# Six groups of value rows summed by TensorE, paired forgetting scores and a fifth late head in a hybrid attention and PEER block

## The reference

```python
h   = x + [ FoX(8 heads of 64) || DiffAttn(4 heads, two maps of 64) ](W_in RMSNorm(x)) @ W_out
h   = h + PEER(RMSNorm(h))
out = RMSNorm_final(h)

# PEER, for each token and each of its 8 heads:
q = (xb @ w_q).reshape(128, 8, 2, 128)            # a block of 128 tokens
sc = einsum('thpd,hpkd->thpk', q, sub_keys)       # two lists of 128 key scores
s1, i1 = top_k(sc[:, :, 0], 16); s2, i2 = top_k(sc[:, :, 1], 16)
top_s, pos = top_k(all 256 sums of s1 and s2, 16) # 16 of 16384 experts
g = softmax(top_s)
hid = gelu(einsum('thkd,td->thk', u_tab[eidx], xb)) * g
out = einsum('thk,thkd->td', hid, v_tab[eidx])
```

## Time and profile before

| | |
|---|---|
| median of 3 runs | 1542.28 us (1540.99 to 1546.88) |
| the profiled execution | 1541.62 us |
| its span, first to last instruction | 1539.8 us |
| TensorE busy | 1269.3 us, 82% |
| VectorE busy | 1077.6 us, 70% |
| ScalarE busy | 459.8 us, 30% |
| GpSimd busy | 751.5 us, 49% |
| DMA | 596.50 MB, mean 387 GB/s |
| granted TensorE clock, mean | 0.939 |

### The profile page before, as it was taken

The page is one execution under the profiler, slowest core; times in us unless marked ns, Lnnn a source line. Parts: engine busy times, 40 slices in busy tenths (PEclk is TensorE's granted clock), DMA queues, the critical chain, the costliest instruction groups (busy, mean ns, idle before and its releaser), DMA issues.

```text
span 1539.8 us, 13062 instructions
## 1 busy us (share of the span) xinstructions
PE 1269.3 (82%) x3727; PEld 658.2 (43%) x3727; DVE 1077.6 (70%) x2520; ACT 459.8 (30%) x1200; POOL 751.5 (49%) x637
## 2 busy tenths in 40 slices
PE   9999999988888488999787777677886787777778
PEld 7766655665545234444333333233332233332333
DVE  3247699999988867566666676666666766666654
ACT  3432355466343022222222222221222222222212
POOL 0016477675667443454544554445444554444440
PEclk9999999999989699999899999989999999999998
DMA  9669799997999999999999999999999999999995
GB/s 382 250 250 413 275 330 351 370 376 268 340 371 392 391 421 416 421 421 421 421 422 422 421 422 421 421 422 421 422 421 421 422 422 421 422 420 422 421 421 208
DMA packets 99741, 596.50 MB, mean 387 GB/s; under 512 B 11480, under 2 KB 11480, under 8 KB 42328
## 3 DMA queue, kind: packets, MB, share of 16 engines
q0 software_dynamic: 89856, 536.91, 86.0%
q1 hardware_dynamic: 9816, 58.77, 9.6%
HBM read 593.54 MB, written 2.10 MB: 387 GB/s over the span
## 4 chain that ended last, share of the span: by engine, by line
DMA 42%; PE 15%; DVE 6%; POOL 3%; issue 2%; ACT 2%; DVEq 0%; POOLq 0%
PE acc L994 13%; DMA map_mem<-in_peer_uv_dram,eidx 10%; DMA w_ring<-in_peer_uv_dram,eidx 9%; DMA v_all<-in_peer_uv_dram,eidx 7%; DMA act_mem<-in_peer_uv_dram,eidx 6%; DMA v_ring<-in_peer_uv_dram,eidx 3%; DMA mix_mem<-in_peer_uv_dram,eidx 3%; DMA u_ring<-in_peer_uv_dram,eidx 3%; DMA v_ring<-in_peer_v_dram,eidx 2%; PE mm L786 1%; ACT diag L1228 1%; DVE map_mem L1549 1%; DVE w_ring L1549 1%; PE sc L786 1%; POOL v_ring L692 1%
## 5 line engine op out<-in xcount | busy, mean ns | idle before, releaser
L1220 ACT ACTIVATE gel<-hid 128x4 f32<-128x4 f32 x126 | 25.8, 205 | 722.2 <-DVE hid L1549 712.5
L685 POOL DMA_INDIRECT u_ring<-in_peer_u_dram,eidx x112 | 136.8, 1221 | 172.9 <-DVE eidx L1529 99.5
L994 PE MATMUL acc<-v_all,diag 128*128 128x512 f32 x256 | 129.2, 651 | 61.1 <-ACT diag L1228 60.6
L692 POOL DMA_INDIRECT v_ring<-in_peer_v_dram,eidx x112 | 133.4, 1192 | 66.4 <-DVE h L1577 38.0
L1577 DVE SCALAR_TENSOR_TENSOR h<-v_ring,coef,h 128x1024 f32<-128x1024 f32 x112 | 143.9, 1284 | 14.3 <-DMA v_ring<-in_peer_v_dram,eidx 11.3
L994 PE MATMUL acc<-map_mem,diag 128*128 128x512 f32 x248 | 123.3, 644 | 32.0 <-ACT diag L1228 32.0
L994 PE MATMUL acc<-v_ring,diag 128*128 128x512 f32 x248 | 120.1, 629 | 32.3 <-ACT diag L1228 28.7
L1541 DVE CUSTOM_DVE_ANT_0 u_ring<-u_ring,hn 128x1024 f32<-128x1024 f32 x112 | 136.6, 1220 | 14.2 <-DMA u_ring<-in_peer_u_dram,eidx 14.0
L994 PE MATMUL acc<-u_ring,diag 128*128 128x512 f32 x248 | 119.1, 626 | 27.4 <-ACT diag L1228 25.8
L1228 ACT ACTIVATE diag<-ident,coef 128x128 f32<-128x128 f32 x392 | 126.3, 390 | 39.1 <-DVE coef L1567 30.8
L711 POOL DMA_INDIRECT v_all<-in_peer_uv_dram,eidx x64 | 76.1, 1189 | 92.3 <-PE acc L994 81.7
(11 more groups left out here) (281 smaller groups left out, 2331.9 us busy)
## 6 DMA issues: line engine op xcount, KB each, us to landing
w_ring<-in_slabs_dram SPq DMA_DIRECT2D x29, 1024.0 KB, 8.4
v_ring<-in_slabs_dram SPq DMA_DIRECT2D x6, 1024.0 KB, 11.2
u_ring<-in_slabs_dram SPq DMA_DIRECT2D x6, 1024.0 KB, 10.9
map_mem<-in_slabs_dram SPq DMA_DIRECT2D x6, 1024.0 KB, 7.9
h<-in_x_dram SPq DMA_DIRECT2D x4, 512.0 KB, 12.5
u_ring<-in_peer_u_dram,eidx POOLq DMA_INDIRECT x112, 6.9
v_ring<-in_peer_v_dram,eidx POOLq DMA_INDIRECT x112, 7.1
v_all<-in_x_cols_dram SPq DMA_DIRECT2D x3, 512.0 KB, 7.4
```

The costliest lines, as they stand in the source:

```text
L685: nc.gpsimd.indirect_dma_start(out=u_ring[:, c % U_RING, :], out_offset=None, in_=peer_u[0], in_offset=bass.IndirectOffsetOnAxis(ap=eidx[n ...
L692: nc.gpsimd.indirect_dma_start(out=v_ring[:, c % V_RING, :], out_offset=None, in_=peer_v[0], in_offset=bass.IndirectOffsetOnAxis(ap=eidx[n ...
L994: last = nc.tensor.matmul(acc[half][:, :], diag[:, c % COLS, :], v_row(n, c)[:, half * BANK:(half + 1) * BANK], start=first, stop=(n % PH ...
L1220: nc.scalar.activation(gel[:, par, g0:g0 + COLS], hid[:, par, g0:g0 + COLS], ACT.Gelu).then_inc(gelu_done, 1)
```

## The change

Three edits.

1. Six of the 28 groups (`SUMMED`, groups 4, 7, 10, 13, 16, 19) are no longer added row by row by VectorE. ScalarE makes four diagonal matrices of the group's coefficients (`sum_diag`), TensorE multiplies the four v rows with them into two of the three rotating banks, and VectorE adds the two banks to `h` (`add_sum`). The piece `sum` stands at gap 0 of slot k + 2; the bank adds stand at gap 1 of the next slot, or before the next output projection's add. The planner gives a sum a share of 10. `row_taken` says which semaphore tells that a v row has been used.
2. The forgetting scores of two neighbouring heads are issued together, at even steps: two products from partitions 0 and 64, then the two gate products.
3. `LATE_HEADS` is 5.

```diff
-LATE_HEADS = 4
+LATE_HEADS = 5
+SUMMED = (4, 7, 10, 13, 16, 19)
+SHARE_SUM = 10.0
...
+    total += SHARE_SUM * len(SUMMED)
+    summed_at = {(k + BEHIND) * GAPS: ("sum", k) for k in SUMMED}
     for p in later:
         k = int(at / total * (SLOTS - 1) * GAPS)
+        while summed_at and k >= min(summed_at):
+            slot = min(summed_at)
+            AFTER[slot].append(summed_at.pop(slot))
+            at += SHARE_SUM
+            k = int(at / total * (SLOTS - 1) * GAPS)
...
+        def row_taken(i):
+
+            if i // COLS in SUMMED and i % COLS == COLS - 1:
+                return mm_full, mm_done(("sum", i // COLS, 1))
+            return added, i + 1 - sum(COLS * k + COLS - 1 <= i for k in SUMMED)
...
             def gather_v(n, c):
                 if n or c >= V_RING:
-                    pool.wait_ge(added, TOPK * n + c + 1 - V_RING)
+                    pool.wait_ge(*row_taken(TOPK * n + c - V_RING))
...
+                elif kind == "sum":
+                    k, = p
+                    pe.wait_ge(*row_taken(COLS * k - 1))
+                    banks = [mm_bank((kind, k, half)) for half in range(2)]
+                    for c in range(COLS):
+                        pe.wait_ge(v_in[c % V_RING], 16 * (k * COLS // V_RING + 1))
+                        pe.wait_ge(sum_diag_done, COLS * SUMMED.index(k) + c + 1)
+                        for half in range(2):
+                            last = nc.tensor.matmul(banks[half][:, :], sum_diag[:, c, :], v_ring[:, c % V_RING, half * BANK:(half + 1) * BANK],
+                                                    start=(c == 0), stop=(c == COLS - 1))
+                            if c == COLS - 1:
+                                last.then_inc(mm_full, 1)
+                        if c < COLS - 1:
+                            last.then_inc(added, 1)
...
+            def pair_scores(g, step):
+
+                t, first = at_step(g, 0, step)
+                nk, j = P * (t + 1), GROUPS[g].index(t)
+                if first == 0:
+                    pe.wait_ge(selq_ready, 2 * (t + 1))
+                both = [(HD * (m % 2), m // 2, map_no[(t, m)]) for m in (first, first + 1)]
+                for lo, ch, k in both:
+                    if k >= len(sc_b):
+                        pe.wait_ge(sc_drained, k + 1 - len(sc_b))
+                    nc.tensor.matmul(sc_b[k % len(sc_b)][:, 0:nk], qT[lo:lo + HD, ch, j * P:(j + 1) * P], kv_t[lo:lo + HD, ch, 0:nk],
+                                     start=True, stop=False)
+                for lo, ch, k in both:
+                    nc.tensor.matmul(sc_b[k % len(sc_b)][:, 0:nk], selq[lo:lo + 40, ch, t % 2, :], caug[lo:lo + 40, 0:nk],
+                                     start=False, stop=True).then_inc(sc_full, 1)
...
+                elif kind == "sum":
+                    n, par, g0 = group_at(p[0])
+                    act.wait_ge(coef_done, p[0] + 1)
+                    if p[0] != SUMMED[0]:
+                        act.wait_ge(mm_full, mm_done((kind, SUMMED[SUMMED.index(p[0]) - 1], 1)))
+                    for c in range(COLS):
+                        nc.scalar.activation(sum_diag[:, c, :], ident[:, :], ACT.Copy,
+                                             scale=coef[:, par, g0 + c:g0 + c + 1]).then_inc(sum_diag_done, 1)
...
                 elif kind == "outproj":
                     g, sl, t = p
+                    if sums_due:
+                        add_sum(sums_due.pop())
...
+            def add_sum(k):
+
+                for half in range(2):
+                    bk = mm_wait(("sum", k, half))
+                    hs = h[:, 0, half * BANK:(half + 1) * BANK]
+                    nc.vector.tensor_tensor(out=hs, in0=bk[:, :], in1=hs, op=ALU.add).then_inc(mm_drained, 1)
...
+                        if gap == 0 and k - BEHIND in SUMMED:
+                            coefs(*behind)
+                            sums_due.append(k - BEHIND)
+                        if gap == 1 and k - BEHIND - 1 in SUMMED and sums_due:
+                            add_sum(sums_due.pop())
...
-                        elif gap < GAPS - 1 and k >= BEHIND:
+                        elif gap < GAPS - 1 and k >= BEHIND and k - BEHIND not in SUMMED:
```

More of the change, by code:

```diff
@@ L303, in build @@
                 MM.append(("fturn", 0))
+        elif kind == "sum":
+            MM += [(*p, half) for half in range(2)]
         elif kind == "turn":
@@ L387, in build @@
         c_all = sb("c_all", [FH, SEQ])
-        z_f = sb("z_f", [FH, max_n])
-        e_f = sb("e_f", [FH, max_n])
+        gate_mem = sb("gate_mem", [P, 2 * max_n])
+        z_f = gate_mem[0:FH, 0:max_n]
+        e_f = gate_mem[0:FH, max_n:2 * max_n]
+        sum_diag = gate_mem[:, 0:COLS * P].rearrange("p (a n) -> p a n", a=COLS)
         selq = mix_mem[:, D:D + FH * P].rearrange("p (a b n) -> p a b n", a=FH // 2, b=2)
@@ L528, in build @@
         added = sem("added")
+        sum_diag_done = sem("sum_diag_done")
         v_used = sem("v_used")
@@ L707, in gather_row @@
                 elif place == FREE_ROWS + 2:
-                    pool.wait_ge(added, HOSTED)
+                    pool.wait_ge(*row_taken(HOSTED - 1))
                 elif place == RING:
@@ L912, in attend @@
                 values(g, half, step)
+            def pair_scores(g, step):
[12 more added lines that the diff above has]
+                                     start=False, stop=True).then_inc(sc_full, 1)
             def scores(g, half, step):
-                if at_step(g, half, step):
+                if half == 0:
+                    if step % 2 == 0 and at_step(g, half, step):
+                        pair_scores(g, step)
+                elif at_step(g, half, step):
                     t, it = at_step(g, half, step)
                     nk, j = P * (t + 1), GROUPS[g].index(t)
-                    if it == 0:
-                        pe.wait_ge(selq_ready, 2 * (t + 1))
                     for m in maps_of(it):
@@ L923, in scores @@
                             pe.wait_ge(sc_drained, k + 1 - len(sc_b))
[L924 to L934, removed]
+                        lo, ch = HD * ((m - FH) % 2), KC // 2 + (m - FH) // 2
+                        nc.tensor.matmul(sc_b[k % len(sc_b)][:, 0:nk], qT[lo:lo + HD, ch, j * P:(j + 1) * P], kv_t[lo:lo + HD, ch, 0:nk],
+                                         start=True, stop=True).then_inc(sc_full, 1)
             def turned_map(g, half, step):
@@ L1296, in _ @@
             handed = [0]
+            sums_due = []
             def link(ins):
@@ L1573, in add_row @@
                 dve.wait_ge(coef_done, GRP * n + c // COLS + 1)
-                if n or c:
-                    dve.wait_ge(added, TOPK * n + c)
+                before = (TOPK * n + c - 1) // COLS
+                if c % COLS == 0 and before in SUMMED:
+                    dve.wait_ge(*emptied(("sum", before, 1)))
+                elif n or c:
+                    dve.wait_ge(*row_taken(TOPK * n + c - 1))
                 ht = h[:, n // PH, :]
```

4 lines of the change are left out of this document (2 added, 2 removed).

## The result

The changed kernel, called after from here on, takes 1581.2 us (median of 4 runs, 1576.5 to 1587.2), the kernel before 1542.0 beside it: ratio 1.025, 95% interval 1.0205 to 1.0295. It is slower, as forecast, but by 39 us and not by 18, and it lies above the range (1578).

What follows compares the result with a forecast made beforehand. VectorE was taken to bound slots 5 to 22 (busy 238.5 of 247.6 us). Terms -21.6 + 45 - 5 + 3 - 1.5 - 4.5 + 2.5 = +17.9 us on 1541.6 gave 1559.5, 1560 against the median; range 1530 to 1578.

Steps and rivals of the forecast that it cites:

- -21.6, the relief: VectorE: 24 adds of 1.20 us go, twelve bank adds of 0.60 us come, net 21.6 us less.
- the walk: Hand pricing of each slot's pieces behind a sum on TensorE, giving 47.6 us of VectorE waiting together.
- rival 1: Sums' slots: VectorE has work enough, waits under 1 us each, the 21.6 us are kept; 1525 us, chance 0.18.
- +45, the new waits: Six sums' slots: TensorE's lead is reset and VectorE waits for pieces behind each sum; 45 us, bounds 0 and 47.6.
- -5, idle time that vanishes: Slots 5 to 22: about 5 of VectorE's 9.1 us idle are no longer there beside the new waits.
- +3: Forgetting gates' product: stands three gaps earlier on VectorE, so three more gaps are left after it, 3 us more.
- -1.5: Tile 0's eight heads, where TensorE bounds: pairing their scores gives 1.5 us.
- -4.5: Slots 24 to 27: one head's queries and a slab less, 54.4 us to 50.
- +2.5: Second stage, DMA-bound: the fifth late head's slab of 1 MB moves there, 2.5 us on the path.
- The pairs: Forgetting scores on TensorE: two heads' products overlap, giving back 17 us of TensorE at most, 0 at least.
- Rival 3: Pairs don't overlap, or only the first products do; TensorE bounds slots 5 to 22; 1572 to 1577 us, chance 0.06.
- Rival 2: Waits eat just what the adds gave, 3.6 to 5 us per sum; 1542 us, 1535 to 1550, chance 0.18.

Runs made afterwards that it cites:

- e6: Changed kernel without any sum, pairs and fifth late head kept, planner leaving the room of six sums empty: 1551.5 us, ratio 1.0058.
- e11: Changed kernel with the sums' products at full width on constants, without waits for VectorE's last add, rows or diagonals (24 rows' part left out): 1553.6 us.
- e15: e11 with each sum product cut from 512 columns to 64: 1550.0 us, ratio 1.006.
- e4: Changed kernel with 64 columns instead of 512 in each sum product, all waits kept: 1574.0 us, ratio 1.023.
- e5: Changed kernel with 4, 11 and 7 unused products ahead of the waits of sums 13, 16 and 19: 1579.8 us, ratio 1.0256.
- e2: Changed kernel with pairs and fifth late head but no sums: 1547.3 us, ratio 1.0044.
- e3: e2 with `LATE_HEADS = 4`, so the pairs alone: 1546.5 us, ratio 1.0037.
- e10: Changed kernel with 18 instead of 10 planner shares for a sum, more empty gaps behind each: 1570.2 us, ratio 1.018.
- e1: Changed kernel with the six sums alone, old unpaired scores and `LATE_HEADS = 4`: 1601.2 us, ratio 1.039.
- e7: Changed kernel with the sum at gap 4, bank adds at gap 5 of the next slot, no wait for VectorE's last add: 1591.2 us.

## Why the prediction was wrong

By the spans the forecast missed 19.0 of 36.9 us: slots 5 to 22 took 12.2 us more than it said (+30.6 for -21.6 + 45 - 5 = +18.4), slot 23 5.4, the second stage 3.6, and the part up to slot 5 and slots 24 to 27 gave back 0.5 and 1.7.

By medians, from kernel to kernel: before 1542.0, pairs 1546.5, late head and placing 1551.5, adds gone and products there 1553.6, TensorE tied to the last add 1556.5, rows and diagonals 1581.2.

**-21.6, the relief: the amount was right, but none of it reached the end.** VectorE's busy time fell by 23.8 us. But from e6 to e11 the time rose by 2, with 24 us more of idle time where no sum waits for a row or a coefficient. I took a stage in which VectorE is busy 238.5 of 247.6 us for one that VectorE alone bounds. GpSimd needs 212 us of it and TensorE 225, and six slots in which VectorE has only 5 to 10 us to do run short of rows (11.5 us in e15) and of projections that wait for the sums' banks (7.9 us). So part of the idle time that I priced as the cost of the waits is relief that this kernel can't use: on the path the waits for rows and coefficients cost 27.6 us (e11 to after), and of the relief nothing arrived. How much would with free banks stays open. The sum hid this, as the walk counted the same idle time once; rival 1 lived on it.

**+45, the new waits: mechanism and place right, size too small.** This is the step that failed. Slot by slot, the walk against the idle time of after: slots 6 and 7 7.0 against 8.5; 9 and 10 3.0 against 5.1; 12 5.6 against 6.8; 15 to 17 11.4 against 17.0; 18 11.1 against 12.2; 21 and 22 9.5 against 11.5. Together 47.6 against 61.1, and I had cut the 47.6 to 45. The term was 16 us too small. What was missing: the sum ends 9.8 us into the slot on average, not 7.7 to 8.8. In part its first product starts 1.7 to 2.2 us into the slot and not 0.8 (slots 6, 12, 15). In part it waits for rows (slots 9, 12, 15): the landing of the last row was counted as one flight of 7.1 us from a free place, but the gather stands in GpSimd's full queue, with one u gather between two v gathers, and where nothing else holds the sum the rows are seen to arrive 2.6 us apart (e4, slot 12). In part it runs at the lower clock, which the walk did not have (2.6 us in slots 18 and 21; e5 took this away and the time did not follow). The largest miss is slots 15 to 17, 5.6 us, where all three meet. After, TensorE, slot 15 begins at 325.9 us:
```profile
327.70 2.05 PE L867 MATMUL mm<-v_ring,gate_mem 128*128 128x512 f32 x2 [4.43 <-DMA v_ring<-in_peer_v_dram,eidx]
329.54 1.74 PE L867 MATMUL acc<-v_ring,gate_mem 128*128 128x512 f32 x2
331.12 1.02 PE L867 MATMUL mm<-v_ring,gate_mem 128*128 128x512 f32 x2
...
335.15 1.13 PE L867 MATMUL mm<-v_ring,gate_mem 128*128 128x512 f32 x2 [0.43 <-DMA v_ring<-in_peer_v_dram,eidx]
```
Behind this sum stand two projections and tile 3's values, and VectorE's wait for these values (7.42 us, until 348.99) follows.

**-5, idle time that vanishes.** Right in kind: outside the slots of that list 2.4 of the 63.5 us are left, of 9.1 in all of slots 5 to 22 before.

**+3, -1.5, -4.5, +2.5.** The +3 for the gates fits: slots 0 to 4 took 83.7 us for 79.4, and 82.5 in e6 without a sum. The -1.5 can't be read: slot 0 began at 106.7 us for 110.1, but over the traces of all kernels that start lies anywhere from 106.7 to 111.4. Slots 24 to 27 gave -6.2 for -4.5, right in kind; slot 23, which I had not counted apart, gave +5.4, and e6 shows that it comes from the placing and not from a sum. The second stage gave +6.1 for +2.5. e2 has 1039.4 us there and e3 1036.7, so the fifth late head is +2.7, as forecast. The rest, 3.7 us, is not tied to the sums' waits: e11 and e15 have most of it (1042.1 and 1042.3), and e10, with six full sums, has none (1039.3). Its cause stays open.

**The pairs.** Priced at 17 us of TensorE, and the rows above agree (1.07 us for two heads where one alone would be 0.96); in slots 5 to 22 its busy time is 214.0 us in e3, for 225.3 before. On the end nothing without the sums (e3). I had set no relief for them beyond tile 0, which was right. With the sums, e1 against after shows 20 us for pairs and late head together, since what stands behind a sum is shorter. Rival 3 (no overlap) is out. The drain that the Trainium skill (TensorEngine Tiling, Key Properties) names for a change of tiling mode shows as no idle time: the last products of the pair start at 215.04 and last 0.37, and the turn of 128 rows starts at 215.35.

**The rivals.** Rival 1 (the 21.6 us are kept) is out by the result, and by e15 for this kernel even without the waits for rows and coefficients. Rival 2 had the right kind of wait and too small a price: it wanted 3.6 to 5 us for each sum to balance the adds, and a sum costs 5 us net of them (1551.5 to 1581.2 for six). The range ended at 1578 because only rival 3 was allowed above the forecast's own 1572 (whose sum gives 1568 to 1577, not 1572 to 1577); the walk itself had no bound for a sum that ends later than 8.8 us.

On order, slot 18 agrees with the Trainium skill (TensorE: Matmul & The Clock Gate, Part 2: What happens when you issue a matmul): nothing of TensorE's queue passed the sum while it waited 10.49 us, and the output projection behind it began at 393.37 with no wait of its own.

## What to carry to other kernels

Taking work from the busiest engine can be worth nothing where others are nearly as full: look at each engine slot by slot, with the 0.3 us of issue before each of GpSimd's gathers counted in, before a relief goes into the sum. Ask as well how long the new work keeps a buffer that others rotate through. An instruction with several producers, put into an in-order queue right where they finish, costs the queue its lead each time; price it by all that stands behind it, with the latest producer's queue in the price. Two waits of the same instruction do not add: undoing either one alone shows less than the pair, so undo both before you judge either. And a run that takes a wait away proves only that wait: read in its trace which ones it left.

## What was not expected of the hardware

- Indirect gathers that GpSimd issues back to back stand 1.24 us apart at best (0.94 busy and 0.30 before). In e7 they waited 43.0 us in all for TensorE to free a v row.
- After TensorE had idled 4.43 us, the first products of 512 columns took 0.92 us each (327.70 to 329.54 for two) and from 331.12 on 0.43. In slot 21, 434.60 to 442.40 us, the granted clock was 0.64 of the full 2.4 GHz on average, after 6.97 us of idle time, so it was for a good part at the lower of its two levels, 1.2 GHz (in slot 15, 325.9 to 336.5 us, it was 0.84). Slot 21, columns as in the earlier trace rows:
```profile
434.60:442.40 7.80, 7.44 (x12) 3.17 (x13) 7.76 (x22) 1.19 (x5) 3.74 (x4) 0.64 0.63 202
```
Keeping TensorE busy with unused products brought the clock to 1.00 in these sums and ended two of them 2.4 and 2.6 us sooner, yet the kernel's time moved by 1.4 us of 1581, within its scatter (e5).
- Products from partitions 0 and 64 overlap for a rank of 40 as for 64: both of 215.04 start together, as do those of 214.28 and 214.29.
